# One kernel, six places changed at once: start, recurrence heads, one-hot rows, both attentions and an arena pad

## The reference, cut to what matters

```python
ada = silu(c) @ ada_w + ada_b                        # 6 x 1024: sh1, sc1, g1, sh2, sc2, g2
u = rms_norm(h, norm1_g) * (1 + sc1) + sh1
zq, zf, zi, zg, zca, zcb, zga, zgb = split(u @ w_in) # each 512 x 1024
f = lb + (1 - lb) * sigmoid(zf)                      # 8 heads of 128
o = hgrn2(q=zq, k=1 - f, v=zi, logf=log(f))          # gated linear recurrence, causal in time
y_a = (rms_norm(o, hg_norm_g) * silu(zg)) @ w_a      # rms over each head's 128
cv = conv31(zca * sigmoid(zcb)); cv = silu(layer_norm(cv, conv_ln_g, conv_ln_b))
h = h + g1 * ((sigmoid(zga) * y_a + sigmoid(zgb) * (cv @ w_b)) @ w_out)
u2 = rms_norm(h, norm2_g) * (1 + sc2) + sh2
h = h + g2 * peer(u2)   # 8 heads: top 16 of 128 x 128 product keys, 16384 experts, gelu, softmax gates
x = rms_norm(h, final_g)
# layer 0: 16 heads of 64 in three dilated groups, relative bias, softmax, groups weighed by their lse
# layer 1: differential attention, 8 heads, two softmaxes of 64 each
p0, p1 = softmax(q0 @ k0.T + bias0), softmax(q1 @ k1.T + bias1)
o = rms_norm_2((p0 - lam_full * p1) @ v, subln_g) * (1 - lambda_init)    # rms over 128
# each: x = x + o @ w_o; x = x + relu(rms_norm_2(x) @ w_in)**2 @ w_out; final rms_norm_2
```

## Time and profile before

| | us |
|---|---|
| median of 3 runs (lowest, highest) | 4153.46 (4152.85, 4156.53) |
| the profiled execution's own time | 4147.71 |
| its span, first to last instruction | 4145.9 |
| TensorE busy | 3811.0 |
| VectorE busy | 2365.9 |
| ScalarE busy | 1355.2 |
| GpSimd busy | 1357.5 |

### The profile page before, as it was taken

How to read it: one execution, slowest core, us unless ns; L and a number is a source line. 1 busy time by engine, 2 the same in 40 slices (tenths; PEclk the granted TensorE clock), 3 DMA queues, 4 the chain that set the end, 5 groups by cost and what they waited for, 6 DMA issues and landing times.

```text
span 4145.9 us, 51694 instructions
## 1 busy us (share of the span) xinstructions
PE 3811.0 (92%) x16940; PEld 2994.4 (72%) x16940; DVE 2365.9 (57%) x4487; ACT 1355.2 (33%) x1872; POOL 1357.5 (33%) x556
## 2 busy tenths in 40 slices
PE   5988798988999999979999998999899989788998
PEld 4887686777878788858888886854688876347886
DVE  4767697516788888437777774035444312655441
ACT  3444232233434344311111112256322234542221
POOL 1111143433343433334444443410244432003442
PEclk8999899999999999989999999999999998789999
DMA  4323322223364645566666652221132222112222
GB/s 166 137 81 127 122 96 66 87 81 107 106 203 121 191 149 164 181 208 181 190 192 182 184 177 72 92 67 35 61 97 97 92 78 91 31 34 76 97 97 76
DMA packets 266636, 486.51 MB, mean 117 GB/s; under 512 B 16721, under 2 KB 148177, under 8 KB 266097
## 3 DMA queue, kind: packets, MB, share of 16 engines
q1 hardware_dynamic: 81936, 299.93, 22.8%
q10 hardware_dynamic: 184580, 184.95, 14.4%
HBM read 415.48 MB, written 84.02 MB: 120 GB/s over the span
## 4 chain that ended last, share of the span: by engine, by line
PE 51%; issue 35%; POOL 11%; DVE 2%; ACT 1%; POOLq 0%; ACTq 0%; DVEq 0%
PE ps L346 14%; PE ps L347 14%; PE ps L348 14%; POOL ring_r L1787 11%; PE ps L646 3%; PE ps L664 3%; PE ps L384 1%; PE ps L654 1%; DVE sq L1283 1%; ACT arena L1127 0%; DVE st L1271 0%; PE ps L691 0%; ACT high_w L762 0%; POOLq L1786 0%; PE ps L628 0%
## 5 line engine op out<-in xcount | busy, mean ns | idle before, releaser
L1787 POOL TENSOR_TENSOR ring_r<-ring,high_w 128x1024 fp32r<-128x1024 f32 x552 | 1357.3, 2460 | 2754.0 <-ACT high_w L762 2186.2
L346 PE MATMUL ps<-uT_r,high_w 128*128 128x512 f32 x2752 | 1103.6, 401 | 102.1 <-DVE sq_r L1288 50.9
L348 PE MATMUL ps<-uT_r,ring_r 128*128 128x512 f32 x2752 | 1081.7, 393 | 0.0
L762 ACT ACTIVATE high_w<-ring 128x1024 fp32r<-128x1024 f32 x424 | 447.1, 1057 | 1101.6 <-PE ps L348 936.7
L347 PE MATMUL ps<-sq_r,high_w 128*128 128x512 f32 x2048 | 803.0, 392 | 0.0
L347 PE MATMUL ps<-part,high_w 128*128 128x512 f32 x1856 | 736.0, 397 | 0.0
L346 PEld LDWEIGHTS ps<-uT_r,high_w 128*128 128x128 f32 x2752 | 523.1, 190 | 225.9 <-issue 75.3
L346 PE MATMUL ps<-part,high_w 128*128 128x512 f32 x1536 | 613.8, 400 | 3.7 <-POOL ring_r L1787 3.7
L348 PE MATMUL ps<-part,ring_r 128*128 128x512 f32 x1536 | 607.6, 396 | 0.0
L348 PEld LDWEIGHTS ps<-uT_r,ring_r 128*128 128x128 f32 x2752 | 521.9, 190 | 115.3
L347 PEld LDWEIGHTS ps<-sq_r,high_w 128*128 128x128 f32 x2048 | 388.7, 190 | 78.1
(11 more groups left out here) (259 smaller groups left out, 4108.0 us busy)
## 6 DMA issues: line engine op xcount, KB each, us to landing
ring<-panels SPq DMA_DIRECT2D x568, 512.0 KB, 3.4
adram<-act_out ACTq DMA_DIRECT2D x128, 256.0 KB, 3.9
gdram<-arena ACTq DMA_DIRECT2D x16, 2048.0 KB, 11.7
arena<-gdram ACTq DMA_DIRECT2D x128, 256.0 KB, 5.9
arena<-adram ACTq DMA_DIRECT2D x128, 256.0 KB, 2.7
arena<-ada_rest ACTq DMA_DIRECT2D x32, 512.0 KB, 4.2
strips_dram<-btab ACTq DMA_DIRECT2D x4, 3584.0 KB
arena<-strips_dram ACTq DMA_DIRECT2D x32, 448.0 KB, 3.3
```

What stands on the lines that cost most here:

```text
L346: t_.matmul(out, wh, xh, start=(k == 0), stop=False)
L348: last = t_.matmul(out, wl, xh, start=False, stop=(k == KT - 1))
L762: s_.activation(high_w[:, j % RING], ring[:, j % RING], ACT.Copy).then_inc(hi_ready, 1)
L1787: g_.tensor_tensor(ring_r[:, j], ring[:, j], high_w[:, j], ALU.subtract).then_inc(lo_ready, 1)
```

## The change

It has these parts, in the order of the program:

- A pad of 24 floats a partition ahead of the arena.
- Start: `cols` has its own semaphore `cols_in`, the tables' loads `tabs_in`; hT's load comes before `blam`, `consts` and `lmask`. The sc1 panels come first. VectorE does panels 0 to 8, 10, 12 and 14, TensorE the odd ones 9 to 15 as products with one weight column (banks 6, 7). ScalarE copies that row, TensorE joins both in the columns' sum. The scaled tiles stand between VectorE's last panels; ScalarE adds the shift and rounds in one pass, VectorE's low part adds the shift itself. ScalarE's high parts of panels 0 to 3 stand behind that pass. The tables are negated.
- The norm before PEER (r = 1) has the same single pass.
- Heads: a Sigmoid in place of exp, addition and reciprocal; the statistic at the head of the step; the root as Ln and Exp(-0.5 x); a level's copy two levels after its factors; level 4 after the fourth panel; head 7 a step like the others, with four gates panels; the gate after the off-diagonal factors; a conditioning set in bank 5.
- One-hot rows: four tokens an instruction, read from PSUM with stride-zero operands.
- Both attentions: the logits are negated, a minimum goes straight to `nm`, no second instruction.
- Attention B: rounds written out by hand; GpSimd stages q, k and v and makes the low parts; one ratio a head in place of two scalings a tile, the norm's epsilon scaled by z0 squared and added by four small products.

The core of the diff:

```diff
+sb("to_128_bytes", [P, 24])
...
+    pe.wait_ge(tabs_in, 32)
...
+    pe.wait_ge(gemm_done, 8)
+    ada_columns(5, lambda o: ada_front[:, 0, o * P:(o + 1) * P])
+    pe.wait_ge(silu_c, 1)
+    for n in range(9, 16, 2):
+        pe.wait_ge(w_slot[n % RING], 16 * (n // RING + 1))
+        for half in range(2):
+            if half:
+                pe.wait_ge(gemm_done, n)
+            last = t_.matmul(ps[0:1, 6 + half, :], small[:, n - 8:n - 7],
+                             ring[:, n % RING, 4 * half:4 * half + 4, :].rearrange("p a b -> p (a b)"),
+                             start=(n == 9), stop=(n == 15))
+        last.then_inc(gemm_done, 1)
+    pe.wait_ge(row_sb, 2)
+    pe.wait_ge(ada_evac, 1)
+    for o in range(8):
+        t_.matmul(ps[:, 5, o:o + 1], ada_front[:, 1, o * P:(o + 1) * P], ones[:, 0:1], start=True, stop=False)
+        last = t_.matmul(ps[:, 5, o:o + 1], ada_row[:, o * P:(o + 1) * P], ones[0:1, 0:1], start=False, stop=True)
+    last.then_inc(ada_done, 1)
+    pe.wait_ge(tab_sb, 4)
...
-    def head_step(h, hh, q8n, jn, before=True, adas=None):
+    def head_step(h, hh, q8n, jn, before=True, adas=None, heads_next=True):
         if hh == 0 and before:
             ada_set(h)
+        if before:
+            head_stat(h - 1 if isinstance(h, int) else h + (-1))
         head_gemm(q8n, jn, 0)
         head_gemm(q8n, jn, 1)
+        if hh == 0 and before:
+            pe.wait_ge(ada_evac, adas)
         head_off(h)
         head_level(h, hh, 0)
-        if hh == 0 and before:
-            pe.wait_ge(ada_evac, adas)
-        if before:
-            head_stat(h - 1 if isinstance(h, int) else h + (-1))
         head_level(h, hh, 1)
-        head_gemm(q8n, jn, 2)
-        for n in (2, 3, 4):
-            head_level(h, hh, n)
+        if heads_next:
+            head_gemm(q8n, jn, 2)
+        else:
+            gates_panel(q8n, jn + 2)
+        head_level(h, hh, 2)
+        head_level(h, hh, 3)
...
         def bstat(u):
+            pe.wait_ge(rs_ms, u + RS_B)
+            pe.wait_ge(bsq_ready, u + 1)
+            pe.wait_ge(zeps_set, u + 1)
+            t_.matmul(ps[:, 7, :], ones[:], sq[:, 0, :], start=True, stop=False)
+            for qt in range(TT):
+                last = t_.matmul(ps[:, 7, qt * P:(qt + 1) * P], zeps[:, u, qt:qt + 1].to_broadcast([P, P]), ident,
+                                 start=False, stop=(qt == TT - 1))
+            last.then_inc(stat_done, 1)
+        def round_b(n):
+            for e in range(2 * TT):
+                if n + 1 < B_HEADS:
+                    logit(n + 1, (n + 1) % 2, e // TT, e % TT)
+                if e < TT and n:
+                    weighted(n - 1, 1 - n % 2, 0, n - 1, e)
+                if e >= TT - 1 and e < 2 * TT - 1:
+                    turn(n % 2, 0, n, e - TT + 1)
+            if n:
+                bstat(n - 1)
...
+    act.dma_start(cc[:], cols).then_inc(cols_in, 16)
+    for dst, src in ((ohs, oh), (rbs[:], rel)):
+        act.dma_start(dst, src).then_inc(tabs_in, 16)
+    act.dma_start(hT[:], xT).then_inc(x_in, 16)
+    for dst, src in ((lam, blam), (cst[:], consts), (lm, lmask)):
         act.dma_start(dst, src).then_inc(c_in, 16)
...
-            for k in range(KT):
-                act.wait_ge(upre, n + k + 1)
-                s_.activation(sq[:, k, :], sq[:, k, :], ACT.Identity,
-                              bias=ada[:, 24 * r + k:24 * r + k + 1]).then_inc(shifted, 1)
+        if r == 0:
+            act.wait_ge(ada_evac, 2)
         for k in range(KT):
+            act.wait_ge(upre, n + k + 1)
             if r < 2:
-                act.wait_ge(shifted, n + k + 1)
+                ins = s_.activation(uT_r[:, k, :], sq[:, k, :], ACT.Identity, bias=ada[:, 24 * r + k:24 * r + k + 1])
             else:
-                act.wait_ge(upre, n + k + 1)
-            s_.activation(uT_r[:, k, :], sq[:, k, :], ACT.Copy).then_inc(x_high, 1)
...
-    for j in range(3):
+    act.wait_ge(gemm_done, 16)
+    for half in range(2):
+        s_.activation(ada_row[:, T * half:T * half + T], ps[0:1, 6 + half, :], ACT.Copy).then_inc(row_sb, 1)
+    high_x(0)
+    for j in range(4):
         high(Q_HEADS, j)
-    high_x(0)
-    high(Q_HEADS, 3)
...
+    def head_log(t):
+        act.wait_ge(rs_ms, t * 1 + (RS_HEAD + 1))
+        s_.activation(sr[:], ms[:], ACT.Ln).then_inc(ms_log, 1)
     def head_root(t):
-        act.wait_ge(rs_ms, t * 1 + (RS_HEAD + 1))
-        s_.activation(rt[:], ms[:], ACT.Abs_reciprocal_sqrt).then_inc(rs_sqrt, 1)
+        act.wait_ge(ms_log, t * 1 + 1)
+        s_.activation(rt[:], sr[:], ACT.Exp, scale=-0.5).then_inc(rs_sqrt, 1)
...
-        s_.activation(eb[:], ps[:, 0, :], ACT.Exp, scale=-1.0).then_inc(bank_free[0], 1)
+        s_.activation(eb[:], ps[:, 0, :], ACT.Sigmoid).then_inc(bank_free[0], 1)
...
+        def copied_b(u):
+            act.wait_ge(a["av_done"], u + 1)
+            s_.activation(sq[:, 1 + u % 2, :], ps[:, 6, :], ACT.Copy).then_inc(a["o_ready"], 1)
+            act.wait_ge(a["o_ready"], u + 2)
+            act.wait_ge(stat_done, u + RS_B)
+            s_.activation(sq[:, 0, :], sq[:, 1 + u % 2, :], ACT.Square).then_inc(bsq_ready, 1)
+        def root_b(u):
+            act.wait_ge(rs_ms, u + (RS_B + 1))
+            s_.activation(sr[:], ms[:], ACT.Ln).then_inc(b_log, 1)
+            act.wait_ge(b_log, u + 1)
+            s_.activation(rt[:], sr[:], ACT.Exp, scale=-0.5).then_inc(rs_sqrt, 1)
...
+        def high_b(u):
+            act.wait_ge(b_out, u + 1)
+            s_.activation(uT_r[:, u, :], act_out[:, 0, :], ACT.Copy).then_inc(b_high, 1)
+        def round_b(n):
+            more = n + 1 < B_HEADS
+            for e in range(2 * TT):
+                if more:
+                    exp(n + 1, (n + 1) % 2, e // TT, e % TT)
+                    if e % TT == TT - 1 and n + 2 < B_HEADS:
+                        strips(2 * n + 4 + e // TT, e // TT)
+                if e == 1 and n >= 2:
+                    root_b(n - 2)
+                if e == TT - 1 and n:
+                    copied_b(n - 1)
+                if e >= TT - 1 and e < 2 * TT - 1:
+                    turned(n % 2, n, e - TT + 1)
+                if e == TT + 1 and n >= 2:
+                    high_b(n - 2)
...
+    def low_x(r):
+        for k in range(KT):
+            ve.wait_ge(x_high, KT * SPLIT_NORM[r] + k + 1)
+            if r < 2:
+                ins = v_.scalar_tensor_tensor(out=(sq_r if r else ulo)[:, k, :], in0=sq[:, k, :],
+                                              scalar=ada[:, 24 * r + k:24 * r + k + 1], in1=uT_r[:, k, :],
+                                              op0=ALU.add, op1=ALU.subtract)
+            else:
+                ins = v_.tensor_tensor(sq_r[:, k, :], sq[:, k, :], uT_r[:, k, :], ALU.subtract)
...
+    for n in (*range(8), *range(8, 16, 2)):
...
-        if n == 11:
+        if n == 4:
+            bounds()
+        if n == 6:
             rsqrt(0, D)
-    for s in range(2):
-        ada_out(s, 5 + s)
+        if n == 8:
+            ada_out(1, 5, done=1)
+            ve.wait_ge(ada_evac, 1)
+            gain_of(0)
+        if n >= 8:
+            for c in {8: (), 10: (0, 1, 2), 12: (3, 4), 14: (5, 6, 7)}[n]:
+                scaled(0, c, lambda k: small[:, 24 + k:25 + k])
+    ada_out(0, 5, done=2)
     ve.wait_ge(ada_evac, 2)
-    gain_of(0)
     ve.wait_ge(tab_dram, 16)
-    norm(0, lambda k: small[:, 24 + k:25 + k])
+    low_x(0)
...
+        def level_out(n):
+            ve.wait_ge(lvl_done, h * 8 + (n + 1))
+            if n:
+                ve.wait_ge(lvl_evac, h * 8 + (n + 1))
+            else:
+                ve.wait_ge(v_free, h * 1 + 1)
+            bank = 7 if n % 2 == 0 else 5
+            carry_waits()
+            v_.copy_predicated(sd[:, hh], lm[:, n, :].unsqueeze(1).broadcast_to([P, TT, P]),
+                               ps[:, bank, :].rearrange("p (a b) -> p a b", a=TT)).then_inc(lvl_evac, 1)
...
+            if n >= 2:
+                level_out(n - 2)
+        for n in (5, 6, 7):
+            level_out(n)
...
+        slotP = ps[:, 4, 0:3 * P].rearrange("p (a b) -> p a b", a=3)
+        with S.loop(16, 4) as i:
             for par in range(2):
                 ve.wait_ge(gmm_done, i * 2 + (tt * 32 + par + 1))
-                for k in range(4):
-                    t = i * 8 + (4 * par + k)
-                    ins = v_.tensor_scalar(arng[:, 4 * par + k, :], iota[:], slotT[:, 0, bass.ds(t, 1)],
-                                           slotT[:, 2, bass.ds(t, 1)], ALU.is_equal, ALU.mult)
-                    ins = v_.tensor_scalar(brng[:, 4 * par + k, :], iota[:], slotT[:, 1, bass.ds(t, 1)], None, ALU.is_equal)
+                four = slice(4 * par, 4 * par + 4)
+                def of_slots(n):
+                    return slotP[:, n, bass.ds(i * 8 + 4 * par, 4)].unsqueeze(2).broadcast_to([P, 4, P])
+                keys = iota.unsqueeze(1).broadcast_to([P, 4, P])
+                S.mark(v_.tensor_tensor(arng[:, four, :], keys, of_slots(0), ALU.is_equal))
```

(62 more changed lines are left out.)

325 lines of the change are left out of this document (130 added, 195 removed).

## The result

The changed kernel takes 4031.57 us (median of 4 runs, 4019.09 to 4038.15) against 4153.16 (4151.10 to 4156.53): a ratio of 0.9709, 95% interval 0.9693 to 0.9725. The forecast was 4031, range 3995 to 4068. The total came out; its parts did not all. The profiled execution is the slowest of the four: own time 4038.15, span 4036.3 against 4145.9, 109.6 less. First its page, parts 1 and 2, to be read against the earlier trace rows.

What follows compares the result with a forecast made beforehand. TensorE, busy 3811 of 4145.9 us, was taken as the bound, with time to gain only where it waits or runs at the lower clock. Savings 12 + 42 + 1.4 + 14 + 53 = 122 from 4153.5 gave 4031 us, range 3995 to 4068.

Steps and rivals of the forecast that it cites:

- Start, -12: Start of the kernel: the heads' first panel comes at 56 instead of 68.16 us, saving 12, between 4 and 20.
- panels 7 and 8: about 30: Start: VectorE at panel 4 until about 20, then panels 5 and 6, root with chain, panels 7 and 8: about 30.
- The two chains alternate by the count of gemm_done, so I take 11: Start: VectorE's four even panels (10.5 with scaled tiles) in step with TensorE's four odd ones, taken as 11 us.
- Heads, -42: Heads: period 48.3 to 43.3 us (41.9 if nothing new waits), plus head 7, convolution, head 0; between -20 and -52.
- 4.66 + 1.4 go: Heads, each period: delayed level copies remove TensorE's 4.66 us wait and 1.4 us at the lower clock.
- VectorE's slack, not TensorE's time: Heads: removing VectorE's reciprocal and addition before f saves TensorE nothing directly, but lets the statistic come early.
- Norm and one-hot rows, -1.4 and -14: Norm before PEER: single ScalarE pass, -1.4 us. One-hot rows: four TensorE waits shortened by 3.5 each, -14, between -6 and -21.
- First attention, 0: First attention: TensorE is at 99%, so no gain; the minimum frees VectorE only.
- fifth rival: Heads and rounds: many short TensorE waits keep the clock at 1.2 GHz; ends near 4318 if all heads do; chance 0.02.
- Second attention, -53: Second attention: 213.3 to 160.6 us with rounds of 18.5, near VectorE's upper end; -70 at 16.1, -28 at 22.
- second rival: Second attention: rounds run at TensorE's sum of 16.1 us, 17 us more gain, total 4014; chance 0.2.
- Pad, 0: Arena pad: no effect, within 4 us either way by the 2 MB stores of 11.7 us.

Runs made afterwards that it cites:

- again: The changed kernel word for word, run once more: median 4029.65 us, ratio 0.9703 against the kernel before.

## Why the prediction was right, and where it was right by chance

- **The sum** (4031) met the median (4031.57); the profiled execution's 4025 met 4038.15. The terms missed by 1.4 to 8.7 us in the table, on either side, and cancelled. That the total came within 1 us is luck.
- **Start, -12: mis-sized, -3.3.** The step that ends "panels 7 and 8: about 30" had no term for the squares' sums; panel 8 began only at 33.57: the 9.66 us of sums begin at 19.05 and not with the landing of hT, as ScalarE is at the tables' copies until 17.8. "The two chains alternate by the count of gemm_done, so I take 11" counted work; the odd panels took 12.3 from 37.22, twice waiting for a load that is only issued when a slot is given back. The rest, from there to the first product, was 15.4 for 13. Eight more executions with this start have -1.8 to -3.1, and again has +1.4, with the lower clock in its last steps.
- **Heads, -42: size right, step wrong.** "4.66 + 1.4 go" was put on the delayed copies. They are worth 0.3 a period and some 6 in head 7. The Sigmoid, costed as "VectorE's slack, not TensorE's time", is worth 4.6 to 6.4 a period, since the early statistic makes f's path TensorE's. The text did say that the Sigmoid is what lets the statistic come early, but costed its absence nowhere. The undisturbed period is 42.0 to 42.1, by my lower bound of 41.9 (whose terms give 42.2) and not the 43.3 I took; the strips' writes gave 15 us of that back. Head 7 gave 7.1 where 4.1 was forecast. The convolution begins 14.8 us after the last copy where 12.6 was forecast, and TensorE's wait before its last mean is 21.3 us and not some 30. That 38 met 42 is therefore partly luck: steps of nearly the right sum, the largest for the wrong reason.
- **Norm and one-hot rows, -1.4 and -14:** TensorE's wait at the norm went from 11.3 to 9.9, which the stretch doesn't show (0.0; -0.2 to -3.0 in the variants); the one-hot stretch has -11.5, each wait 2.5 where 2.2 was forecast. The three instructions take 681 to 687 ns, not held. Right by its own steps.
- **First attention, 0:** +7.4 in the profile, the clock of its first 27 us; between -3.1 and +8.4 over the profiled executions. This is the fifth rival in small: one wait of 2.6 us and not many short ones.
- **Second attention, -53:** -61.0, or -58.6 to the tile held last. The round is 17.5 and not 18.5, and TensorE sets it at 16.8, the second rival's mechanism with its sum of 16.1 a little low. I had taken VectorE's upper end with half of GpSimd's 2.4 for each of five instructions; GpSimd's copies take 0.61 to 0.90 and VectorE is busy for 11.8 of 17.5. My sum for ScalarE was also added up wrongly: its terms give 16.0 and not 14.7, and the trace has 13.3. The Trainium skill ("ScalarE: Activation LUTs", Table sets) has one load for a logarithm and an exponential; the round's trace still shows two of 1.28, and they don't matter, for ScalarE's 13.3 us lie beside TensorE's 16.8.
- **Pad, 0:** about -13. The bound of 4 us from the stores' 11.7 was drawn too narrow. My estimate from the Trainium skill ("DMA: Bandwidth & Descriptors", How a descriptor splits into AXI transactions), by which the pad was to cost up to 18% of a store, doesn't fit: the store went from 11.7 to 10.3 or less.

Spread: the changed kernel's runs lie within 19 us, those of the kernel before within 5.4. Between executions the lower clock's share moves attention A by 7.6 us, attention B by 4 to 7 and the first product by 5.

## What to carry to other kernels

A wait that has two causes queued behind each other is priced by undoing each part alone and both together; a term called slack needs the question what the same change moves ahead of it. Bulk DMA writes that are not needed for milliseconds belong where TensorE has slack, since one late panel, taken up in order by ScalarE, costs the wait, all that is queued behind it and the lower clock after. In rounds shared by three engines, count the engine with the largest busy sum first, here within 1.5 us of the measured round. And where the clock's dips differ between executions of one program, a difference of a few us between two profiles is not yet one between two kernels.

## What the hardware showed that was not expected

- A shift of the arena's address by 96 bytes a partition changed the 2 MB stores from 11.7 us to between 9.6 and 10.3 and, by the medians, the kernel by 12.8 to 14.7 us. Why is not shown.
- TensorE's granted clock was at the lower of its two levels (1.2 and 2.4 GHz) for 3.4 to 27.3 us behind the same 2.62 us wait, at the longest with TensorE busy throughout (27.79 of 27.80 us).
- A four-token VectorE instruction with both operands in SBUF ended 0.55 us after GpSimd's whenever it started inside one (63 of 63, up to 2.83 us long) and took 0.69 otherwise; with one operand in PSUM it took 0.69 either way.
